# Three bfloat16 parts for the expert scatter-add, a halved hand-over behind the loop, and a norm shift on ScalarE

## What is computed

```
def rms_norm(x, g):
    y = x * lax.rsqrt(jnp.mean(x * x, axis=-1, keepdims=True) + EPS)
    return y * g
def modulate(x, g, shift, scale):
    return rms_norm(x, g) * (1 + scale[:, None, :]) + shift[:, None, :]
def swiglu(x, w_g, w_u, w_d):
    return (jax.nn.silu(x @ w_g) * (x @ w_u)) @ w_d
# routed experts: for each block of up to 128 tokens of one expert e
out = swiglu(x[toks], w_gate[e], w_up[e], w_down[e]) * wr[:, None]
y   = y.at[toks].add(out)
# layer: x = x + gate * (y + swiglu(x, shared weights)); then the next norm
```

## Time and profile before

| | us |
|---|---|
| median of 3 runs | 1849.35 |
| lowest, highest | 1846.43, 1854.1 |
| the profiled execution, its own time | 1847.61 |
| its span, first to last instruction | 1845.7 |
| PE busy | 1693.6 (92%) |
| DVE, ACT, POOL busy | 413.8, 434.3, 164.8 |
| expert loops with their overflow | 363.5 to about 937, and 1268.5 to about 1821 |

### The profile page before, as it was taken

How to read it: one execution, slowest core, us unless ns; L and a number is a source line. 1 busy time by engine, 2 the same in 40 slices (tenths; PEclk the granted TensorE clock), 3 DMA queues, 4 the chain that set the end, 5 groups by cost and what they waited for, 6 DMA issues and landing times.

```text
span 1845.7 us, 28458 instructions
## 1 busy us (share of the span) xinstructions
PE 1693.6 (92%) x11144; PEld 983.8 (53%) x11144; DVE 413.8 (22%) x1341; ACT 434.3 (24%) x944; POOL 164.8 (9%) x229
## 2 busy tenths in 40 slices
PE   5999888799999999999988957789999999999996
PEld 4677465455455454454446735665555454554554
DVE  3123544050000000000032864255300000000003
ACT  1111020122222222222221124121222222222222
POOL 0001200000000000000010333001000000000000
PEclk8999698899999999999989978799999999999998
DMA  9865545999999999999570411085999999999970
GB/s 360 327 226 176 207 160 213 408 371 370 412 403 401 402 392 394 399 395 399 210 285 1 138 59 46 0 302 206 378 390 402 409 394 402 395 397 407 395 315 24
DMA packets 139029, 552.34 MB, mean 299 GB/s; under 512 B 19408, under 2 KB 36638, under 8 KB 104663
## 3 DMA queue, kind: packets, MB, share of 16 engines
q1 hardware_dynamic: 120562, 513.82, 71.0%
q0 software_dynamic: 15392, 34.66, 5.3%
q10 hardware_dynamic: 3012, 3.00, 0.5%
HBM read 562.74 MB, written 8.60 MB: 310 GB/s over the span
## 4 chain that ended last, share of the span: by engine, by line
PE 77%; DVE 7%; DMA 3%; ACT 1%; issue 1%; SPq 0%; DVEq 0%; POOLq 0%; POOL 0%; ACTq 0%
PE PS L1277 26%; PE PS L1242 14%; PE PS L1306 13%; PE PS L1234 4%; PE PS L787 3%; PE PS L1246 2%; PE PS L1790 2%; DMA ring<-in_w_ada 2%; PE PS L1794 2%; PE PS L1829 1%; PE PS L1290 1%; PE PS L1169 1%; PE PS L439 1%; PE PS L500 1%; PE PS L759 1%
## 5 line engine op out<-in xcount | busy, mean ns | idle before, releaser
L1277 PE MATMUL PS<-ring,arena 128*64 128x256 f32 x4288 | 490.6, 382 | 4.5 <-DMA ring<-in_moe_w_down 2.9
L1277 PEld LDWEIGHTS PS<-ring,arena 128*64 128x64 f32 x4288 | 304.4, 137 | 185.7 <-issue 43.2
L1242 PE MATMUL PS<-arena 128*128 128x512 f32 x536 | 266.4, 621 | 0.0
L1485 DVE TENSOR_TENSOR arena<-arena,PS 128x128 f32<-128x128 f32 x134 | 38.5, 288 | 989.7 <-ACT arena L1550 989.7
L1306 PE MATMUL PS<-ring,arena 128*64 128x512 f32 x1072 | 259.6, 605 | 0.7 <-ACT arena L1552 0.7
L1242 PEld LDWEIGHTS PS<-arena 128*128 128x128 f32 x536 | 91.5, 190 | 113.0 <-issue 112.9
L1560 ACT COPY arena<-PS 64x512 f32<-64x512 f32 x134 | 77.5, 578 | 239.6 <-PE PS L1306 239.6
L1580 POOL COPY arena<-arena 128x1 int32 (+1 forms) x71 | 14.5, 204 | 1245.3 <-PE PS L1234 1018.3
L1306 PEld LDWEIGHTS PS<-ring,arena 128*64 128x64 f32 x1072 | 65.0, 136 | 113.8 <-issue 77.8
L1550 ACT ACTIVATE arena<-PS 128x128 f32<-128x128 f32 x134 | 37.2, 278 | 321.8 <-PE PS L1277 321.8
L1234 PEld LDWEIGHTS PS<-cst,arena 128*128 128x128 f32 x552 | 71.8, 192 | 75.7 <-issue 73.9
(11 more groups left out here) (468 smaller groups left out, 1398.7 us busy)
## 6 DMA issues: line engine op xcount, KB each, us to landing
ring<-in_moe_w_gate SPq DMA_DIRECT2D x134, 1024.0 KB, 4.9
ring<-in_moe_w_up SPq DMA_DIRECT2D x134, 1024.0 KB, 7.2
ring<-in_moe_w_down SPq DMA_DIRECT2D x134, 1024.0 KB, 9.3
ring<-in_w_ada SPq DMA_DIRECT2D x32, 1152.0 KB
ring<-in_w_ada SPq DMA_DIRECT2D x16, 768.0 KB
ring<-in_gla_w_in SPq DMA_DIRECT2D x8, 1152.0 KB
ring<-in_dsa_w_in SPq DMA_DIRECT2D x6, 1024.0 KB
arena<-in_state_gla POOLq DMA_DIRECT2D x8, 512.0 KB, 5.9
```

Source lines behind the costliest of these rows:

```text
L1242: ins_ = pe.matmul(PS[:, c, :], OH[par][:, T * P:(T + 1) * P], ysb[par][:, 512 * j:512 * j + 512], start=False, stop=True, skip_group_chec ...
L1277: m = pe.matmul(PS[64 * half:64 * half + 64, 5, 0:256].rearrange("p (g n) -> p g n", g=2), rows[:, k, CAP * b:CAP * b + CAP], gu[:, :, k, ...
L1485: dve.tensor_tensor(hm[b], sg[b], PS[:, 5, P:2 * P], ALU.mult).then_inc(M(l, "hm"), 1)
```

## The change

Five things change.

1. The scatter-add. `OH` becomes a plain 0/1 one-hot in bfloat16. DVE splits the weighted rows of `ysb` into three bfloat16 parts `yw[0..2]` that sum to the float32 value (`dve_rows`, one half of 512 columns at a time), and PE adds the three parts one after the other (`pe_add`). DVE makes the first half at the start of the next pair's first expert, ahead of its silu product, and the second half behind that product and the one-hot.
2. The order of the chunks. First expert: the first half turn of the gathered rows comes directly behind the gate and up product, the turn of `hm` after it, then chunks 0 and 2 (column half 0), which are what the first half of the split feeds. Second expert: chunks 1 and 3. In the overflow loop the order is chunks 0 and 2 ahead of the down product and 1, 3, 4 behind it, and DVE instead of ACT copies the second half turn.
3. The last pair of a layer keeps the float32 add, with a one-hot `OHw` of its own.
4. Behind the loop ACT copies banks 2 and 3 too, DVE's wait for the last gathers moves behind the sums, `ffn_added` is counted for both token halves, squares, their sum, root and reciprocal go by halves of 128 and 136 columns.
5. In the three tile-wise norms ACT adds the shift (`act_shift`), DVE only scales; the sample tokens' columns are counted in `h_tail`.

```diff
-        OH = [tk(TOK) for _ in range(2)]
+        OH = [tk(TOK, dt=BF16) for _ in range(2)]
+        OHw = tk(TOK)
+        yw = arena[:, 0:3 * D // 2].bitcast(BF16).rearrange("p (c n) -> p c n", c=3)
...
-        def pe_add(par, parts):
+        def pe_add(oh, rows, parts):
 
             for c in parts:
...
+                T, j = c // 2, c % 2
+                for y in rows:
+                    if c < 4:
+                        ins_ = pe.matmul(PS[:, c, :], oh[:, T * P:(T + 1) * P], y[:, 512 * j:512 * j + 512],
+                                         start=False, stop=True, skip_group_check=True)
+                        continue
...
             m.then_inc(M(l, "gu"), 1)
             if isinstance(n, int):
                 pe_between(l, n)
-            if over:
-                if b == 0:
-                    add(0, 1)
-            elif b == 0:
-                add(0, 1)
-            else:
-                add(2, 3)
-            pe.wait_ge(M(l, "hm"), n + 1)
-            pe.transpose(PS[:, 5, 256:384], hm[b], K["ident"]).then_inc(M(l, "th"), 1)
-            if over and b == 0:
-                add(2, 3, 4)
-            elif over:
-                pe_turn_half(l, h2 + 1, 1, i + NE // 4, 0)
-            elif b == 0:
+            if not over and b == 0:
                 if isinstance(n, int):
                     pe_bank6(l, n)
                 pe_turn_half(l, h2 + 1, 1 - par, i + par, 0)
+            elif not over:
+                add(1, 3)
+            pe.wait_ge(M(l, "hm"), n + 1)
+            pe.transpose(PS[:, 5, 256:384], hm[b], K["ident"]).then_inc(M(l, "th"), 1)
+            if over and b == 1:
+                pe_turn_half(l, h2 + 1, 1, i + NE // 4, 0)
+            elif b == 0:
+                add(0, 2)
             else:
                 add(4)
...
+        def dve_rows(l, par, m, j):
+
+            q = slice(512 * j, 512 * j + 512)
+            if j == 0:
+                dve.wait_ge(M(l, "ysb"), m * 2 + 2)
+                if not isinstance(m, int) or m >= 1:
+                    dve.wait_ge(M(l, "added"), m)
+            part = M(l, "part")
+            dve.tensor_scalar(yw[:, 0, q], ysb[par][:, q], wv[:, par:par + 1], None, ALU.mult).then_inc(part, 1)
+            dve.wait_ge(part, m * 6 + (3 * j + 1))
+            dve.scalar_tensor_tensor(out=ysb[par][:, q], in0=ysb[par][:, q], scalar=wv[:, par:par + 1], in1=yw[:, 0, q], op0=ALU.mult, op1=ALU.subtract).then_inc(part, 1)
+            dve.wait_ge(part, m * 6 + (3 * j + 2))
+            dve.tensor_copy(yw[:, 1, q], ysb[par][:, q]).then_inc(part, 1)
+            dve.wait_ge(part, m * 6 + (3 * j + 3))
+            dve.tensor_tensor(yw[:, 2, q], ysb[par][:, q], yw[:, 1, q], ALU.subtract).then_inc(M(l, "split"), 1)
...
+        def act_shift(n, l, part):
+
+            shift = modT2[:, l, 24 * part:24 * part + 8, :]
+            for k in range(KT):
+                act.wait_ge(S("h_scaled"), KT * (n - 1) + k + 1)
+                act.activation(hT[:, k, 0:SEQ], hT[:, k, 0:SEQ], ACT.Identity, bias=shift[:, k, 0:1]).then_inc(S("h_ready"), 1)
```

More of the change, by code:

```diff
@@ L510, in dve_rms @@
         def dve_rms(n):
-            dve.wait_ge(S("x_rms"), n + 1)
+            if n % 2 == 0 and n:
+                for h in range(2):
+                    dve.wait_ge(S("x_rms"), n + (n // 2 - 1) + h + 1)
+                    ins_ = dve.reciprocal(rstd[:, COLS[h]], rstd[:, COLS[h]])
+                dv(ins_)
+                return
+            dve.wait_ge(S("x_rms"), n + n // 2 + 1)
             dv(dve.reciprocal(rstd[:], rstd[:]))
@@ L1308, in pe_body @@
             m.then_inc(M(l, "y"), 1)
-            if over and b == 1:
+            if over and b == 0:
+                add(1, 3, 4)
+            elif over:
                 pe_turn_half(l, h2 + 1, 1, i + NE // 4, 1)
@@ L1483, in body @@
                 par = 1 if over else u // 2
+                last = None if b or isinstance(h2, int) and h2 == 0 else h2 - 1
+                if last is not None:
+                    dve_rows(l, 1 if over else 1 - par, last, 0)
                 dve.wait_ge(M(l, "sg"), n + 1)
@@ L1561, in body @@
                 act.copy(ysb[par][q, 512:D], PS[CAP:P, 7, :]).then_inc(M(l, "ysb"), 1)
-                if turns:
+                if turns and not over:
                     evict_half(h2 + 1, into, 1)
```

123 lines of the change are left out of this document (73 added, 50 removed).

## The result

The changed kernel takes 1792.3 us (median of 4 runs, 1788.5 to 1795.5) against 1847.9 for the kernel before on the same chip: a ratio of 0.969, 95% interval 0.966 to 0.972. In a later comparison it was 1789.5 us (5 runs) and 0.968 (0.966 to 0.970). The prediction was 1791, range 1778 to 1812. All times and ratios here are of fast runs; one run of the kernel with the gather wait first, 1851.4 us at a granted clock of 0.90 where its others have 0.95, is left out as a slow one. The profiled execution took 1790.99 us, its span is 1789.1.

The account below looks back on a forecast made before the run. PE, not the weight stream, was taken as the bound. 48 (loops) + 6.4 (behind the loop) + 2.5 (shift) = 57 us off the profiled 1847.6 gave 1790.6, stated as 1791 us, range 1778 to 1812.

Parts of the forecast that it names:

- The stream: Expert-loop weight loads: with a never-empty queue 15.7 us a pair at 418 GB/s; PE starts each expert 14.4 us in hand.
- Rival (e): Expert loop: wide bfloat16 matmul 0.13 us, PE needs 14.7 a pair, weight stream binds at 15.7; 1759 us; chance 0.02.
- The matmuls: Scatter-add on PE: a wide bfloat16 matmul takes 0.217 us, so two chunks take 1.30 us instead of 1.82.
- (d): Scatter-add on PE: a bfloat16 matmul costs its upper bound, 0.256 us; 30 us more, 1821 us; chance 0.05.
- Second expert: Second expert of a pair in the loop: PE takes 7.42 us instead of 7.94, the cheaper sample chunk counted as nothing.
- First expert: First expert of a pair: 8.33 us instead of 8.53, with 0.32 us open wait ahead of the turn of hm.
- DVE's split: Ahead of DVE's product in the first expert: first half takes 2.47 us, hidden with 0.09 us to spare before silu ends.
- (b): DVE's split: multiply and cast run at single slope, hm 0.45 us late in some 65 pairs; 1820 us; chance 0.08.
- (c): DVE's split, ahead of the first expert's product, is the bound: 5.7 us at strided pace; 1995 us; chance 0.03.
- Sums over the loops: Both layers' expert loops, overflow included: 48 us saved, 40 of it from 28 pairs a layer at 0.72 us each.
- Behind the loop: Sums, squares, root and reciprocal after the experts: 3.1 us saved in layer 1, 3.3 in layer 0, together 6.4.
- The shift: Tile-wise norms: DVE loses 24 instructions, 8.2 us in all; saving taken as 2.5 us, bounds 0 and 8.2.

Follow-up runs that it names:

- gather wait first: Changed kernel with DVE's wait for the last gathers of rows put back ahead of the sums behind the loop: 1787.9 us, ratio 0.967.
- longer second half: Changed kernel with the last subtraction of DVE's split made twice in the second half of each pair's split: 1789.7 us, ratio 0.967.
- the kernel with two parts: Changed kernel with PE adding only two of the three bfloat16 parts, DVE still making the third, so the sum is less exact: 1771.9 us, ratio 0.959.
- the float32 kernel in the new order: Changed kernel with the float32 add again, no split on DVE, chunks kept in their new places: 1857.5 us, ratio 1.004.
- longer first half: Changed kernel with the last subtraction of DVE's split made twice in the first half of each pair's split: 1827.7 us, ratio 0.987.
- the kernel without the shift: Changed kernel with DVE scaling and shifting again and ACT adding nothing in the norms: 1791.4 us, ratio 0.967.
- new add alone: Kernel before with only the three-part add, its chunk order and the last pair's float32 add; combine and norms untouched: 1799.4 us, ratio 0.972.

## Why the prediction was right, point by point

**What bounds.** Right. PE's row set the pair, and taking 0.74 us from it took 0.74 from the time. The longer second half shows that DVE's work as such costs nothing.

**The stream.** The floor of 15.7 us was right: 15.43 and 14.87 could be held only while a lead lasted. The bandwidth rose to 413 GB/s, near the 415 foretold. The lead of 14.4 us was wrong by more than half. It rested on the landing of one slot's loads in the overflow, 10.3 us, and in the loop of the changed kernel the down load takes 16.4; it also took a slot as refilled at the end of its expert, where the down load is issued 1.3 us later. For the forecast this did not matter, since PE's 15.73 is still above the floor. Rival (e) came out too low for it: the kernel with two parts, with PE at 14.87 where (e) has 14.7, took 1772 us and not 1759.

**The matmuls.** 0.215 us for 0.217. The Trainium skill ("TensorE: Matmul & The Clock Gate", Back-to-back issue gap) gives an isolated gap of about 216 ns for 512 columns and says that a sustained stream reaches 131. The stream here agrees with the first figure and not with the second: 0.215 us in the rows of L1273. Rivals (d) and (e) fall with it.

**Second expert.** 7.32 us for 7.42. Gate and up with chunks 1 and 3 took 4.92 us for 4.90; the 0.10 lies between the turn of `hm` and down, 0.63 us and not the 0.75 of before. The prediction let ACT's copy set the 0.75 and costed the cheaper sample chunk at nothing; the float32 kernel in the new order has 0.75 there again, so it was the chunk.

**First expert.** 8.41 for 8.33. Gate and up to the turn of `hm` 4.32 as foretold, the open wait 0.36 for 0.32; from the turn to down 1.58 for 1.50, down and the second half turn 2.51 as before. The errors of the two experts cancel: 15.73 for 15.75.

**DVE's split.** 2.45 us for 2.47, each of the four instructions within 0.01 us; 0.08 us ahead of silu for 0.09. The run with the longer first half puts the real room at 0.18. Rivals (b) and (c) are out: the multiply took 0.48 and the dense cast 0.43 us. Each microsecond beyond the room cost 38 / 0.54 = 70 us there, for the 65 with which (c) reckoned.

**Sums over the loops.** 48 foretold, 26.0 + 21.2 = 47 in the two expert stages of the table and 2 more on to ACT's copy of layer 0, where the last float32 chunks took 3.70 us at a granted clock of 1.00, for 5.40 at 0.68 before. The overflow of layer 0 gave its share otherwise than argued. The wait of 2.92 us for weights went, and what came next was DVE, which now copies the second half turn there:

```profile
890.73 3.67 PE L1310 MATMUL PS<-ring,arena 128*64 128x256 f32 x32 [1.13 <-DVE arena L1546]
```

**Behind the loop.** Layer 1: 3.24 us for 3.1. Layer 0: 14.49 to 10.93 us, 3.6 for 3.3, in the kernel without the shift; in the changed kernel itself 14.49 to 13.71, since the standstill took 2.8 of it back. The prediction had no term for that. The wait for the gathers was counted as a small item on top. In the chain it is worth 2.2 us (wait back in place) to 3.2 us (new add alone), but the total of the kernel with the wait back in place does not show it.

**The shift.** 2.8 us in the norm ahead of layer 1's router, for 2.5 in all; in layer 0 it shortened the same stretch by 1.7 (13.3 to 11.6 us), and the stage behind it gave that back (363.5 before, 359 to 370 in the executions with the shift). The norm ahead of layer 1's mixer gained nothing, since PE's products there take longer than the tiles: in the changed kernel the first 32 matmuls of that mixer run to 933.8 us, and the last of the eight tiles is ready at 930.1. The total shows none of this; in the profiled executions the standstill cancels it.

So the terms for the loops and the shift were each right by their own rows, the one behind the loop was 4.0 us for 6.4 in the changed kernel, and a loss of 2.8 us that no row of before contained is the reason. That the forecast still came within 2 us is partly luck: what was measured, 56 and 61 us in the two comparisons, doesn't tell 57 from 54.

## What to carry to other kernels

Trading DVE time for PE time pays where PE's row has no idle time, and the place counts for more than the amount: the same 0.72 us was worth 38 us ahead of the product for which PE waits and nothing behind it. When moved work uncovers a wait, fill it with what is already there (here a quarter of the wide add: 10 us more in the expert stages), and ask next what the stream still allows: one counter raised by several loads gives the lead of the load that lands last. After a gain, look at waits on things that nobody needs, such as a last prefetch: this one cost 0.2 us in layer 0 until the new add made PE early, and 3.2 then.

## What the runs showed of the hardware

- The same dense add of 512 columns takes PE 0.43 us for each of two float32 instructions and 0.215 us for each bfloat16 one, so three bfloat16 parts (0.65 us) undercut one float32 chunk (0.86).
- With PE waiting for weights, the kernel with two parts moves 415 to 417 GB/s in every full slice of its loops but the last. The kernel before moved 398, with dips to 156 behind a refill, and the changed kernel 413. So 398 was no limit of the memory; that the dips are a queue run dry fits this and was not tested by itself.
- One further wait on a computed value ahead of PE's down product cost 0.12 us a pair, and nothing once the wait of the second expert stood ahead of the sample chunk: pairs are back at 15.43 us, as without any further wait.
- DVE can stand still for 2.1 to 2.7 us in the combine with "remote" as the only releaser, in both executions of one kernel and the single ones of five others, and not in those of four more, at equal work. Differences of 3 us between two kernels can come from that alone.
